# Scores of two attention heads as two 64-row tiles, spread over three steps

## Chip, cores and metric

The kernel runs on one core of one Trainium2 chip. The metric is the device time of one execution in microseconds; lower is better.

## What is computed

One inference step of a two-layer decoder trunk with 512 new prompt tokens and 8 samples that continue a cache of 2048 tokens each. Layer 1 is a gated linear attention (GLA), layer 2 a stick-breaking attention over shared keys and values. The change touches only the stick-breaking attention of the prompt tokens (16 heads of 64 features), which is, for each head:

```python
z = einsum('bqhd,bkhd->bhqk', q, k) * 64**-0.5 + bias_h
mask = k_pos[None, :] < pos[:, None]
log_keep = where(mask, log_sigmoid(-z), 0.0)
later = cumsum(log_keep, reverse=True) - log_keep
a = where(mask, exp(log_sigmoid(z) + later), 0.0)
o = einsum('bhqk,bkhd->bqhd', a, v)          # then o * silu(gate), and @ w_out
```

In the kernel `a` is the product of sigmoid(z) with a running product, taken from the right, of sigmoid(-z).

## The kernel before

Every engine has one program, written out by hand, and semaphores order them. The stages follow one another: projections and GLA, output and embedding layers, then the query, gate, K and V projections of layer 2 (`g1`, `K`, `V`), the attention of the prompt, the output product `wo1` and the last gate `ple1`. From the K stage on, TensorE also multiplies the cached value pages of the samples: `value_quad` takes four pages (512 KB each) from a ring of eight slots that SP refills; four 32-column tiles run side by side. There are 32 such groups of four; the last 16 stand in the attention stage, two per pair of heads. `sample_features` turns the result of two samples into features and stands three times in the stage or at its edge.

The attention stage works by heads. The 512 queries are four blocks of 128, and block q sees (q+1)*128 keys, so a head has 128+256+384+512 = 1280 score columns. For each head:

- **scores** (TensorE, L1954): the query block, padded with zeros over the 64 rows of the other head of its pair (`qz`, copied by ScalarE in `pair_queries`, zeroed by GpSimd), times the keys `K1T`, into banks 1 (block 1), 0 (blocks 0 and 2) and 2 (block 3). A bf16 mask matmul (L1950) goes first in each block.
- **head_sigmoids** (ScalarE, L960 and L963): sigmoid(-z) into `pcum` and sigmoid(z) into `psig`, bank by bank.
- **head_scans** and **head_products** (VectorE, L1450 and L1459): the reversed running product in `pcum`, then `psig` times `pcum`.
- **weights_back** (TensorE, L1968): ten 128x128 blocks of `psig` are turned into banks 3, 4 and the upper half of bank 1.
- **head_weights** (ScalarE, L1010 to L1012): these are copied to `pat`.
- **values** (TensorE, L1981), once per pair: `V1` times `pat` as two 64-column tiles into bank 5.
- **gate_pair** (VectorE, L1464): bank 5 times the gate `g1T`.

The order on TensorE is, for head h: scores(h+1), weights_back(h), four pages, and after an odd head values of the pair. At the end come `sample_features(3)`, the turned embedding rows of layer 2 (L1863) after the gate of the last pair, and `wo1` (L1585), whose input `g1T` is split in a high part (ScalarE, `x_hi`) and a low part (VectorE, `x_lo`).

Of the kernel before, what the change touches and what calls it, by code (L numbers as in the profile page):

```python
# [12 lines left out]
P = 128  # L13
# [39 lines left out]
X_SETS = ("A", "B", "A", "B", "B", "B", "A")  # L53
# [54 lines left out]
ZBANKS = ((1, 256, (1,)), (0, 512, (0, 2)), (2, 512, (3,)))  # L108
ZB = {0: (0, 0), 2: (0, P), 1: (1, 0), 3: (2, 0)}
# [5 lines left out]
PAIR_AT = {0: 2, 1: 3, 2: 4, 4: 5, 6: 6, 8: 7}  # L115
AB = {0: (3, 0), 1: (4, 0), 3: (4, 384), 2: (1, 256)}
AO = {0: 0, 1: 512, 3: 896, 2: 1024}
# [98 lines left out]
def build(nc, x_prompt, x_sample, state_gla, cache_k, cache_v, page_table, p_prompt, p_sample,  # L216
# [3 lines left out]
    with ExitStack() as ctx:  # L220
# [22 lines left out]
        w_hi = [new(f"w_hi{i}", [P, 1024], F32R) for i in range(2)]  # L243
        w_lo = [new(f"w_lo{i}", [P, 1024], F32R) for i in range(2)]
# [100 lines left out]
        pin1 = at("pin1", [P, TB, PLE], F32, offA)  # L345
        ps1 = at("ps1", [NS, PLE], F32, offA + size([P, TB, PLE]))
        ystage = at("ystage", [P, TB, D], F32, offB)
        ysrow = at("ysrow", [NS, D], F32, offB + size([P, TB, D]))
# [6 lines left out]
        psig = [at(f"psig{i}", [P, NZ], F32, offB + i * pz) for i in range(2)]  # L355
# [4 lines left out]
        qz = [at(f"qz{i}", [P, 2, NP_TOK], F32, off_split + (0, 2, 1, 3)[i] * 4096) for i in range(4)]  # L360
# [94 lines left out]
        def _(sp):  # L455
# [79 lines left out]
            sp.wait_ge(S("z_p"), len(ZBANKS) * SH)  # L535
# [18 lines left out]
        def _(pool):  # L554
# [66 lines left out]
            for i in range(4):  # L621
                pool.wait_ge(S("mm"), last_tile("V") - (1 if i < 2 else 0))
                nc.gpsimd.memset(qz[i][HD:P, 0, :], 0.0)
                nc.gpsimd.memset(qz[i][0:HD, 1, :], 0.0).then_inc(S("qz_zero"), 1)
# [5 lines left out]
        def _(act):  # L630
# [322 lines left out]
            def head_sigmoids(h):  # L953
                if h >= 2:
                    act.wait_ge(S("at_t"), h - 1)
                for e, (bk, cols, blocks) in enumerate(ZBANKS):
                    act.wait_ge(S("z_p"), h * len(ZBANKS) + e + 1)
                    for q in blocks:
                        c0, n = ZB[q][1], (q + 1) * P
                        nc.scalar.activation(pcum[h % 2][:, SEG[q]:SEG[q] + n], bank[bk][:, c0:c0 + n], ACT.Sigmoid,  # L960
                                             bias=nbiasbc[:, h:h + 1], scale=-HD ** -0.5)
                    p0 = PSEG[blocks[0]]
                    nc.scalar.activation(psig[h % 2][:, p0:p0 + cols], bank[bk][:, 0:cols], ACT.Sigmoid,  # L963
                                         bias=biasbc[:, h:h + 1], scale=HD ** -0.5).then_inc(S("sig_p"), 1)

            def pair_queries(i):

                if i < 4:
                    act.wait_ge(S("mm"), last_tile("V") - (1 if i < 2 else 0))
                else:  # L970
                    act.wait_ge(S("z_p"), len(ZBANKS) * 2 * (i - 3))
                nc.scalar.copy(qz[i % 4][0:HD, 0, :], q1T[0:HD, i, :])
                nc.scalar.copy(qz[i % 4][HD:P, 1, :], q1T[HD:P, i, :]).then_inc(S("qz"), 1)

            for i in range(24):
# [21 lines left out]
                if i == 23:  # L997
                    pair_queries(0)
                    head_sigmoids(0)
# [4 lines left out]
            pair_queries(1)  # L1004

            def head_weights(h):
                act.wait_ge(S("at_t"), h + 1)
                if h >= 2:
                    act.wait_ge(S("o_p"), h // 2)
                nc.scalar.copy(pat[h % 2][:, 1024:1280], bank[1][:, 256:512])  # L1010
                nc.scalar.copy(pat[h % 2][:, 512:1024], bank[4])
                nc.scalar.copy(pat[h % 2][:, 0:512], bank[3]).then_inc(S("at_act"), 1)  # L1012

            for h in range(SH):
                if h + 1 < SH:
                    head_sigmoids(h + 1)
                head_weights(h)
                if h in PAIR_AT:
                    pair_queries(PAIR_AT[h])
                if h == 12:  # L1020
                    act.wait_ge(S("z_p"), len(ZBANKS) * 12)
                    split_hi(PHASES["wo1"][0])

            act.wait_ge(S("o_p"), SH // 2)
            act.wait_ge(S("v_st"), 16)
            act.dma_start(w_up1[:, :, :], w_ple_up[1].rearrange("(k p) n -> p k n", p=P)).then_inc(S("up_in"), 16)
            act.wait_ge(S("so1_used"), NS // 2)
            act.wait_ge(S("u1_out"), KT)
            for i in range(KT):
                x_hi(5 * KT + i, g1T[:, i, :])  # L1030
# [41 lines left out]
        def _(dve):  # L1072
# [370 lines left out]
            def head_scans(h):  # L1443
                C = pcum[h % 2]
                for e, (_, _, blocks) in enumerate(ZBANKS):
                    dve.wait_ge(S("sig_p"), h * len(ZBANKS) + e + 1)
                    for q in blocks:
                        n, s = (q + 1) * P, SEG[q]
                        rev = C[:, s + n - 1:s - 1:-1] if s else C[:, n - 1::-1]
                        own.did(nc.vector.tensor_tensor_scan(rev, rev, ones[:, 0:1].to_broadcast([P, n]), 1.0,  # L1450
                                                             ALU.mult, ALU.mult))

            def head_products(h):
                A, C = psig[h % 2], pcum[h % 2]
                own.wait()
                for q in range(TB):
# [3 lines left out]
                last.then_inc(S("a_p"), 1)  # L1460
# [6 lines left out]
            head_scans(0)  # L1467
            sample_gate(1)
            head_products(0)
            for h in range(SH):  # L1470
                if h == 8:
                    sample_rows(2)
                if h % 2 == 0 and h:
                    gate_pair(h // 2 - 1)
                if h + 1 < SH:
                    head_scans(h + 1)
                    if h == 8:
                        sample_gate(2)
                    head_products(h + 1)
                if h == 12:  # L1480
# [4 lines left out]
            for i in range(KT):  # L1485
# [31 lines left out]
        def _(pe):  # L1517
# [418 lines left out]
            def scores(h):  # L1936

                i = h // 2
                if h == 0:
                    pe.wait_ge(S("evac"), last_tile("V"))  # L1940
                pe.wait_ge(S("qz"), i + 1)
                pe.wait_ge(S("qz_zero"), min(i + 1, 4))
                if h >= 2:
                    pe.wait_ge(S("at_act"), h - 1)
                for e, (bk, _, blocks) in enumerate(ZBANKS):
                    if h:
                        pe.wait_ge(S("sig_p"), (h - 1) * len(ZBANKS) + e + 1)
                    for q in blocks:
                        c0, n = ZB[q][1], (q + 1) * P
                        nc.tensor.matmul(bank[bk][:, c0 + n - P:c0 + n], identb[:], maskneg[:],  # L1950
                                         start=(q != 2), stop=False, skip_group_check=True)
                    for q in blocks:
                        c0, n = ZB[q][1], (q + 1) * P
                        last = nc.tensor.matmul(bank[bk][:, c0:c0 + n], qz[i % 4][:, h % 2, q * P:(q + 1) * P],  # L1954
                                                K1T[:, i, 0:n], start=False, stop=True, skip_group_check=True)
                    last.then_inc(S("z_p"), 1)

            def weights_back(h):

                pe.wait_ge(S("a_p"), h + 1)  # L1960
                if h:
                    pe.wait_ge(S("at_act"), h)
                for kb in (0, 1, 3, 2):
                    bk, c0 = AB[kb]
                    if bk == ZBANKS[0][0] and h + 1 < SH:
                        pe.wait_ge(S("sig_p"), (h + 1) * len(ZBANKS) + 1)
                    for q in range(kb, TB):
                        last = nc.tensor.transpose(bank[bk][:, c0 + (q - kb) * P:c0 + (q - kb + 1) * P],  # L1968
                                                   psig[h % 2][:, PSEG[q] + kb * P:PSEG[q] + (kb + 1) * P], ident[:])
                last.then_inc(S("at_t"), 1)  # L1970

            def values(i):

                pe.wait_ge(S("at_act"), 2 * i + 2)
                if i:
                    pe.wait_ge(S("u1_out"), i)
# [36 lines left out]
            for i in range(24):  # L2013
# [14 lines left out]
                if i == 23:  # L2028
                    scores(0)
# [6 lines left out]
            for h in range(SH):  # L2036
                if h + 1 < SH:
                    scores(h + 1)
                if h == 0:
                    pe.wait_ge(S("kv_out"), 16)  # L2040
                if h == 8:
                    sample_features(2)
                weights_back(h)
                value_quad(QUAD * (16 + h))
                if h % 2:
                    values(h // 2)
            sample_features(3)
# [52 lines left out]
```

## Time and profile before

| | |
|---|---|
| median of 3 runs | 896.98 us (896.32 to 899.54) |
| the profiled execution | 896.06 us, of which the span of the records is 894.3 us |
| TensorE busy | 855.4 us, 96% of the span |
| VectorE busy | 544.3 us, 61% |
| ScalarE busy | 449.9 us, 50% |
| GpSimd busy | 282.0 us, 32% |
| share of TensorE in the chain that ended last | 80% |
| memory traffic | 232.5 MB, mean 260 GB/s |

Busy time counts an engine's own instructions and not its waits. The chain is followed back from the last instruction, at each step to what released it. A matmul of 4-byte data leaves two records on TensorE, and records of a pipelined engine overlap, so the distance from start to start tells the cost and not the length of one record. A window's row gives the stretch, its length, the busy us (and instructions) of TensorE, its weight loads, VectorE, ScalarE and GpSimd, and then TensorE's granted clock as a share of full speed, the mean busy share of the DMA engines and GB/s.

### The profile page before, as it was taken

To read this page: it belongs to the slowest core of one execution; us is meant where nothing else is said; L and a number is where in the kernel's file an instruction comes from. 1 tells how busy PE (TensorE), PEld (TensorE's weight loads), DVE (VectorE), ACT (ScalarE), POOL (GpSimd) and SP (SyncE) were. 2 spreads that over 40 slices of the span, in tenths; PEclk is the share of its full clock that TensorE was granted. 3 is DMA by queue.
4 is the path that set the end of the run, shared out by engine and by line. 5 is a ranking of instruction groups with operands and counts; after the bars stand their busy time and mean duration, and the time that the engine had idled before them with its cause. 6 is when DMAs were issued, how large, how long until landed. Compare 5 with 4: busy or idle time off the path is not lost.

```text
span 894.3 us, 14799 instructions
## 1 busy us (share of the span) xinstructions
PE 855.4 (96%) x5069; PEld 596.0 (67%) x5069; DVE 544.3 (61%) x672; ACT 449.9 (50%) x1498; POOL 282.0 (32%) x150
## 2 busy tenths in 40 slices
PE   5999999999899999999999999999989999999995
PEld 3556667877654444454488877877744554899994
DVE  4455385788866879979992722312367777653643
ACT  5501382245567687758863411221387766434433
POOL 3000000957786999995830000000100000020110
PEclk9999999999999999999999999999999999999997
DMA  9898978665589998988992089988798788221202
GB/s 334 281 376 283 396 242 282 217 221 207 171 297 380 383 362 315 336 316 311 348 383 88 1 292 354 355 295 312 284 339 306 269 309 327 95 95 48 95 1 95
DMA packets 109306, 232.48 MB, mean 260 GB/s; under 512 B 7409, under 2 KB 66424, under 8 KB 109232
## 3 DMA queue, kind: packets, MB, share of 16 engines
q1 hardware_dynamic: 50736, 171.64, 52.8%
q10 hardware_dynamic: 58496, 59.90, 20.0%
q8 instruction: 40, 0.66, 0.3%
q14 instruction: 34, 0.28, 0.1%
HBM read 220.38 MB, written 11.14 MB: 259 GB/s over the span
## 4 chain that ended last, share of the span: by engine, by line
PE 80%; DMA 7%; DVE 6%; ACT 4%; issue 1%; SPq 1%; POOL 0%; ACTq 0%; DVEq 0%; POOLq 0%
PE pp L1572 18%; PE pp L1585 18%; PE pp L1588 12%; PE pp L1997 6%; PE pp L1569 4%; PE pp L1954 4%; DMA s<-in_state_gla_dram 3%; DMA slot<-in_cache_v_dram 2%; PE pp L1981 2%; PE pp L1549 2%; PE pp L1968 2%; PE pp L1600 2%; PE pp L1665 1%; PE pp L1612 1%; DMA slot<-in_w_ple_gate_dram 1%
## 5 line engine op out<-in xcount | busy, mean ns | idle before, releaser
L611 POOL TENSOR_TENSOR slot<-slot,qb 128x1024 f32<-128x1024 f32 x96 | 251.0, 2645 | 89.1 <-DMA slot<-in_cache_k_dram 53.8
L1258 DVE TENSOR_REDUCE zall<-slot 128x16 f32<-128x1024 f32 x100 | 120.1, 1214 | 23.9 <-POOL slot L611 22.8
L1081 DVE TENSOR_TENSOR w_lo<-w_raw,w_hi 128x1024 fp32r<-128x1024 f32 x57 | 79.4, 1394 | 71.5 <-ACT w_hi L661 71.3
L803 ACT ACTIVATE slot<-slot 128x64 f32<-128x64 f32 x448 | 107.1, 241 | 23.4 <-POOL slot L611 23.4
L661 ACT CAST w_hi<-w_raw 128x1024 fp32r<-128x1024 f32 x58 | 60.5, 1045 | 60.1 <-PE pp L1588 26.4
L1588 PE MATMUL pp<-xa_hi,w_hi 128*128 128x512 f32 x200 | 82.1, 411 | 4.6 <-DVE w_lo L1081 4.6
L1572 PE MATMUL pp<-xn,w_raw 128*128 128x512 f32 x192 | 84.3, 593 | 0.5 <-ACT xn L672 0.5
L803 ACT ACTIVATION_READ_ACCUMULATOR slot<-slot 128x1 f32 x448 | 84.1, 188 | 0.0
L1572 PE MATMUL pp<-xn,w_unsplit 128*128 128x512 f32 x192 | 83.9, 592 | 0.0
L1588 PE MATMUL pp<-xa_hi,w_lo 128*128 128x512 f32 x200 | 79.3, 396 | 0.0
L1588 PE MATMUL pp<-xa_lo,w_hi 128*128 128x512 f32 x200 | 79.2, 396 | 0.0
L1585 PE MATMUL pp<-xb_hi,w_hi 128*128 128x260 f32 x384 | 78.8, 286 | 0.2 <-DVE w_lo_k L1081 0.2
L1585 PE MATMUL pp<-xb_lo,w_hi 128*128 128x260 f32 x384 | 77.2, 283 | 0.0
L1585 PE MATMUL pp<-xb_hi,w_lo 128*128 128x260 f32 x368 | 74.3, 283 | 0.0
L1257 DVE TENSOR_TENSOR slot<-slot,qb 128x1024 f32<-128x1024 f32 x32 | 66.5, 2080 | 0.0
L1572 PEld LDWEIGHTS pp<-xn,w_unsplit 128*128 128x128 f32 x192 | 36.5, 190 | 44.2 <-issue 44.0
L1572 PEld LDWEIGHTS pp<-xn,w_raw 128*128 128x128 f32 x192 | 36.1, 190 | 44.4 <-issue 43.5
L1450 DVE TENSOR_TENSOR_SCAN pcum<-pcum,ones 128x256 f32<-128x256 f32 (+1 forms) x64 | 49.3, 812 | 24.8 <-ACT psig L963 24.8
L1997 PE MATMUL pp<-slot,zs 128*32 128x512 f32 x480 | 61.5, 598 | 1.6 <-DMA slot<-in_cache_v_dram 0.9
L1585 PEld LDWEIGHTS pp<-xb_hi,w_hi 128*128 128x128 f32 x384 | 59.0, 189 | 1.8 <-issue 0.8
L1585 PEld LDWEIGHTS pp<-xb_lo,w_hi 128*128 128x128 f32 x384 | 59.1, 188 | 0.0
L1585 PEld LDWEIGHTS pp<-xb_hi,w_lo 128*128 128x128 f32 x368 | 56.7, 188 | 0.0
(304 smaller groups left out, 1438.2 us busy)
## 6 DMA issues: line engine op xcount, KB each, us to landing
slot<-in_cache_k_dram SPq DMA_DIRECT2D x128, 512.0 KB, 5.9
slot<-in_cache_v_dram SPq DMA_DIRECT2D x120, 512.0 KB, 5.7
w_raw<-in_gla_w_in_dram ACTq DMA_DIRECT2D x12, 1024.0 KB, 7.1
slot<-in_gla_w_in_dram SPq DMA_DIRECT2D x24, 512.0 KB, 11.0
w_raw<-in_w_kv_dram ACTq DMA_DIRECT2D x8, 1024.0 KB, 10.4
w_raw<-in_w_ple_gate_dram ACTq DMA_DIRECT2D x6, 1024.0 KB, 5.7
s<-in_state_gla_dram SPq DMA_DIRECT2D x1, 4096.0 KB, 27.5
out_dram<-s ACTq DMA_DIRECT2D x4, 1024.0 KB, 8.4
```

What stands on the lines that cost most here:

```text
L611: nc.gpsimd.tensor_tensor(slot[s][:], slot[s][:], qb[:, (n // NPG) % 2, :], ALU.mult).then_inc(S("k_mul_pool"), 1)
L661: nc.scalar.copy(hi, raw).then_inc(S("w_hi"), 1)
L803: ins = nc.scalar.activation(part, part, ACT.Copy, accum_out=zall[:, n % NPG, b * SH + h:b * SH + h + 1])
L1081: nc.vector.tensor_tensor(lo, raw, hi.bitcast(F32), ALU.subtract).then_inc(S("w_split"), 1)
L1257: own.then(nc.vector.tensor_tensor(at, at, qb[:, b % 2, :], ALU.mult))
L1258: nc.vector.tensor_reduce(zall[:, n % NPG, b * SH:(b + 1) * SH], at.rearrange("p (h d) -> p h d", d=HD), AX.X, ALU.add).then_inc(S("k_used ...
L1450: own.did(nc.vector.tensor_tensor_scan(rev, rev, ones[:, 0:1].to_broadcast([P, n]), 1.0, ALU.mult, ALU.mult))
L1569: last = nc.tensor.matmul(pp[m % 2][:, t, 0:H2], w[:, k, :], x[:, t * H2:(t + 1) * H2], start=(k == 0), stop=(k == KT - 1))
L1572: last = nc.tensor.matmul(bank[banks_of(j)[0]], w[:, k, :], x[:, 0:NP_TOK], start=(k == 0), stop=(k == KT - 1))
L1585: last = nc.tensor.matmul(pp[m % 2][:, t, 0:H2], w[:, k, :], x[:, t * H2:(t + 1) * H2], start=(k == 0 and first), stop=(k == KT - 1 and w ...
L1588: last = nc.tensor.matmul(bank[banks_of(j)[0]], w[:, k, :], x[:, 0:NP_TOK], start=(k == 0 and first), stop=(k == KT - 1 and w is wl))
L1997: last = nc.tensor.matmul(pp[3][32 * g:32 * g + 32, t, :], zs[:, c:c + 32], slot[SLOT_OF[e0 + g]][:, t * 512:(t + 1) * 512], start=(j0 == ...
```

## The change

Scores are made for a pair of heads at once. The query is read from `q1T` directly; head 0 of the pair sits in rows 0 to 63, head 1 in rows 64 to 127, and their matmuls are 64-row tiles into different banks. A pair's scores come in three steps: block 3 into banks 0 and 2, blocks 0 and 2 into the same two, block 1 into banks 1 and 5. ScalarE and VectorE follow these steps. Four sets of `psig` are kept in place of two; the third lies over split weights (`w_hi1`, `w_lo1`), the fourth over `work` and `sqacc`, the staging row of the K and V outputs of the samples. `qz`, its copies and its memsets are gone. The order on TensorE for pair p becomes: step 0 of p, values of p-2, turned weights of head 2p-2, steps 1 and 2 of p, four pages, turned weights of head 2p-1, four pages. Turned weights of the last head go to banks 0, 2 and 1. `wo1` reads its input from the set A region and `ple1` from B (before: B and A), and the high and low parts of the first seven tiles of `wo1`'s input now stand ahead of the gate of the last pair on VectorE.

```diff
-X_SETS = ("A", "B", "A", "B", "B", "B", "A")
+X_SETS = ("A", "B", "A", "B", "B", "A", "B")
-ZBANKS = ((1, 256, (1,)), (0, 512, (0, 2)), (2, 512, (3,)))
+HSTEPS = (((3,), (0, 2)), ((0, 2), (0, 2)), ((1,), (1, 5)))
+ZCOL = {0: 0, 2: P, 1: 0, 3: 0}
+SIG_AT = {(0, 0): 1, (0, 1): 2, (1, 0): 3, (2, 0): 4, (1, 1): 5, (2, 1): 6}
+AB_LAST = {0: (0, 0), 1: (2, 0), 3: (2, 384), 2: (1, 0)}
...
-        psig = [at(f"psig{i}", [P, NZ], F32, offB + i * pz) for i in range(2)]
+        psig_at = (offB, offB + pz, off_split + 8192, off_work + 2 * size([P, T]))
+        psig = [at(f"psig{i}", [P, NZ], F32, o) for i, o in enumerate(psig_at)]
...
-            sp.wait_ge(S("z_p"), len(ZBANKS) * SH)
+            sp.wait_ge(S("at_t"), SH - 2)
             sp.dma_start(pin1[:, :, :], ...)
...
+            def sigmoids(p, e, x):
+                h = 2 * p + x
+                blocks, banks = HSTEPS[e]
+                if e == 0 and x == 0:
+                    if p:
+                        act.wait_ge(S("a_first"), p)
+                    if p >= 2:
+                        act.wait_ge(S("at_t"), 2 * (p - 1))
+                if e == 1 and p:
+                    act.wait_ge(S("a_p"), h - 1)
+                act.wait_ge(S("z_p"), 6 * p + 2 * e + x + 1)
...
+            act.wait_ge(S("kv_ss"), 64)
+            for p in range(PAIRS + 1):
+                if 0 < p < PAIRS:
+                    sigmoids(p, 0, 0)
+                    sigmoids(p, 0, 1)
+                if p:
+                    head_weights(2 * p - 2)
+                if p < PAIRS:
+                    for x in range(2):
+                        sigmoids(p, 1, x)
+                        sigmoids(p, 2, x)
+                if p == PAIRS - 2:
                     split_hi(PHASES["wo1"][0])
+                if p:
+                    head_weights(2 * p - 1)
...
+            def first_blocks(p):
+                for x in range(2):
+                    dve.wait_ge(S("sig_p"), 6 * p + SIG_AT[0, x])
+                    scans(x, (3,))
+                own.wait()
+                products(p, 0, (3,))
+                products(p, 1, (3,)).then_inc(S("a_first"), 1)
+            def other_blocks(p, x):
+                dve.wait_ge(S("sig_p"), 6 * p + SIG_AT[1, x])
+                scans(x, (0, 2))
+                dve.wait_ge(S("sig_p"), 6 * p + SIG_AT[2, x])
+                scans(x, (1,))
+                own.wait()
+                products(p, x, (0, 2, 1)).then_inc(S("a_p"), 1)
...
+            for p in range(PAIRS):
+                if p == PAIRS // 2:
+                    sample_rows(2)
+                if p:
+                    first_blocks(p)
+                if p == PAIRS // 2:
+                    sample_gate(2)
+                if p >= 2:
+                    gate_pair(p - 2)
+                other_blocks(p, 0)
+                other_blocks(p, 1)
             sample_rows(3)
-            gate_pair(SH // 2 - 1)
+            gate_pair(PAIRS - 2)
             sample_gate(3)
-            for i in range(KT):
+            for i in range(KT - 1):
                 x_lo(5 * KT + i, g1T[:, i, :])
+            gate_pair(PAIRS - 1)
+            x_lo(6 * KT - 1, g1T[:, KT - 1, :])
...
+            def scores(p, e):
+                blocks, banks = HSTEPS[e]
+                if e == 0:
+                    if p:
+                        pe.wait_ge(S("sig_p"), 6 * (p - 1) + SIG_AT[1, 1])
+                    else:
+                        pe.wait_ge(S("evac"), last_tile("V"))
+                if e == 1:
+                    pe.wait_ge(S("sig_p"), 6 * p + SIG_AT[0, 1])
+                if e == 2:
+                    if p:
+                        pe.wait_ge(S("sig_p"), 6 * p)
+                        pe.wait_ge(S("at_b1"), 2 * p - 1)
+                    else:
+                        pe.wait_ge(S("kv_out"), 16)
+                    if p >= 2:
+                        pe.wait_ge(S("u1_out"), p - 1)
+                for x in range(2):
                     for q in blocks:
+                        c1 = ZCOL[q] + (q + 1) * P
+                        nc.tensor.matmul(bank[banks[x]][:, c1 - P:c1], identb[:], maskneg[:],
                                          start=(q != 2), stop=False, skip_group_check=True)
+                for q in blocks:
+                    c0, n = ZCOL[q], (q + 1) * P
+                    for x in range(2):
+                        r = x * HD
+                        ins = nc.tensor.matmul(bank[banks[x]][:, c0:c0 + n], q1T[r:r + HD, p, q * P:(q + 1) * P],
+                                               K1T[r:r + HD, p, 0:n], start=False, stop=True, skip_group_check=True)
...
+            for p in range(PAIRS):
+                if p:
+                    scores(p, 0)
+                if p >= 2:
+                    values(p - 2)
+                if p == PAIRS // 2:
                     sample_features(2)
+                if p:
+                    weights_back(2 * p - 2)
+                scores(p, 1)
+                scores(p, 2)
+                value_quad(QUAD * (16 + 2 * p))
+                if p:
+                    weights_back(2 * p - 1)
+                value_quad(QUAD * (17 + 2 * p))
+            values(PAIRS - 2)
+            weights_back(SH - 2)
             sample_features(3)
+            weights_back(SH - 1)
+            values(PAIRS - 1)
```

## Rows read from the trace of the kernel before

**Rows 1.** Windows of the attention stage: from:to, length, then each engine.
```profile
679.30:693.10 13.80, 13.62 (x95) 7.01 (x94) 10.25 (x17) 10.38 (x22) 0.00 (x0) 1.00 0.90 319
...
665.50:750.20 84.70, 83.49 (x572) 43.97 (x570) 63.59 (x105) 61.18 (x129) 0.00 (x0) 1.00 0.86 306
```

**Rows 2.** Timeline of TensorE over one head: start, us, engine, line, operation, tiles.
```profile
679.25 0.23 PE L1950 MATMUL pp<-maskneg,identb 128*128 128x128 bf16 x1
679.32 0.65 PE L1954 MATMUL pp<-K1T,qz 128*128 128x256 f32 x2
...
681.81 1.26 PE L1968 MATMUL pp<-ident,psig 128*128 128x128 f32 x10
682.99 1.92 PE L1997 MATMUL pp<-slot,zs 128*32 128x512 f32 x16
685.10 0.22 PE L1950 MATMUL pp<-maskneg,identb 128*128 128x128 bf16 x1 [0.18 <-issue]
```

**Rows 3.** The chain that ended last, from the attention stage on: start, us, what.
```profile
643.15 0.16 PE pp L1950
...
657.51 0.22 PE pp L1950
...
690.76 2.36 PE pp L1981 x16
...
764.95 0.18 DVE g1T L1394
...
766.73 46.33 PE pp L1585 x384
```

**Rows 4.** Timeline of TensorE around the 64-row state products, and four full-array blocks.
```profile
184.16 2.00 PE L1821 MATMUL pp<-vtok,kdtok 64*128 64x256 f32 x16
186.09 0.50 PE L1588 MATMUL pp<-xa_hi,w_hi 128*128 128x512 f32 x1
...
252.41 1.89 PE L1828 MATMUL pp<-vtok,attT 128*128 128x256 f32 x8
```

**Rows 5.** Timeline of ScalarE over the sigmoids and copies of one head.
```profile
680.06 0.47 ACT L960 ACTIVATE pcum<-pp,nbiasbc 128x256 f32<-128x256 f32 x1 [3.17 <-PE pp L1954]
680.44 0.47 ACT L963 ACTIVATE psig<-pp,biasbc 128x256 f32<-128x256 f32 x1
681.04 0.84 ACT L960 ACTIVATE pcum<-pp,nbiasbc 128x128 f32<-128x128 f32 x2
...
682.34 0.70 ACT L960 ACTIVATE pcum<-pp,nbiasbc 128x512 f32<-128x512 f32 x1
...
683.48 0.40 ACT L1010 COPY pat<-pp 128x256 f32<-128x256 f32 x1
...
684.68 0.64 ACT L972 COPY qz<-q1T 64x512 f32<-64x512 f32 x1
```

**Rows 6.** Groups of VectorE by form (busy us, mean ns), then its timeline over one head.
```profile
L1450 DVE TENSOR_TENSOR_SCAN pcum<-pcum,ones 128x512 f32<-128x512 f32 x16 | 19.2, 1200 | 0.0
...
L1459 DVE TENSOR_TENSOR psig<-psig,pcum 128x512 f32<-128x512 f32 x16 | 10.9, 682 | 0.0
...
679.37 0.69 DVE L1464 TENSOR_TENSOR g1T<-pp,g1T 128x512 f32<-128x512 f32 x1 [0.71 <-PE pp L1981]
...
682.49 2.39 DVE L1450 TENSOR_TENSOR_SCAN pcum<-pcum,ones 128x128 f32<-128x128 f32 x3 [0.86 <-ACT psig L963]
684.91 1.70 DVE L1459 TENSOR_TENSOR psig<-psig,pcum 128x128 f32<-128x128 f32 x4
```

**Rows 7.** Timeline of SP's page issues.
```profile
647.76 0.33 SPq L508 DMA_DIRECT2D work<-in_cache_v_dram  x1
...
685.12 8.35 SPq L508 DMA_DIRECT2D slot<-in_cache_v_dram  x7
```

**Rows 8.** DMA issues, 643.3 to 648 and 742 to 752: KB, median landing.
```profile
work<-in_cache_v_dram SPq DMA_DIRECT2D x1, 512.0 KB, 6.0
...
slot<-in_cache_v_dram SPq DMA_DIRECT2D x7, 512.0 KB, 6.5
```

More of the change, by code:

```diff
@@ L242, in build @@
         off_split = top[0]
-        w_hi = [new(f"w_hi{i}", [P, 1024], F32R) for i in range(2)]
-        w_lo = [new(f"w_lo{i}", [P, 1024], F32R) for i in range(2)]
+        w_hi, w_lo = zip(*[(new(f"w_hi{i}", [P, 1024], F32R), new(f"w_lo{i}", [P, 1024], F32R)) for i in range(2)])
         off_work = top[0]
@@ L966, in pair_queries @@
[L966 to L973, printed above, removed]
+            def sigmoids(p, e, x):
[9 more added lines that the diff above has]
+                act.wait_ge(S("z_p"), 6 * p + 2 * e + x + 1)
+                z, A, C = bank[banks[x]], psig[2 * (p % 2) + x], pcum[x]
+                for q in blocks:
+                    c0, n = ZCOL[q], (q + 1) * P
+                    nc.scalar.activation(C[:, SEG[q]:SEG[q] + n], z[:, c0:c0 + n], ACT.Sigmoid,
+                                         bias=nbiasbc[:, h:h + 1], scale=-HD ** -0.5)
+                p0, cols = PSEG[blocks[0]], sum((q + 1) * P for q in blocks)
+                nc.scalar.activation(A[:, p0:p0 + cols], z[:, 0:cols], ACT.Sigmoid, bias=biasbc[:, h:h + 1],
+                                     scale=HD ** -0.5).then_inc(S("sig_p"), 1)
@@ L997, in _ @@
                 if i == 23:
-                    pair_queries(0)
-                    head_sigmoids(0)
+                    sigmoids(0, 0, 0)
+                    sigmoids(0, 0, 1)
                 if i >= KV_LAG + 8:
@@ L1003, in _ @@
                 kv_tile(t)
-            pair_queries(1)
             def head_weights(h):
@@ L1441, in _, with scans, products @@
                     own.did(nc.vector.memset(pcum[i][:, c:c + 1], 1.0))
[L1443 to L1456, printed above, removed]
+            def scans(x, blocks):
+                C = pcum[x]
+                for q in blocks:
+                    n, s = (q + 1) * P, SEG[q]
+                    rev = C[:, s + n - 1:s - 1:-1] if s else C[:, n - 1::-1]
+                    own.did(nc.vector.tensor_tensor_scan(rev, rev, ones[:, 0:1].to_broadcast([P, n]), 1.0,
+                                                         ALU.mult, ALU.mult))
+            def products(p, x, blocks):
+                A, C = psig[2 * (p % 2) + x], pcum[x]
+                for q in blocks:
                     n, s = (q + 1) * P, SEG[q]
@@ L1956, in scores @@
-                    last.then_inc(S("z_p"), 1)
+                for q in blocks:
+                    c0, n = ZCOL[q], (q + 1) * P
+                    for x in range(2):
+                        r = x * HD
+                        ins = nc.tensor.matmul(bank[banks[x]][:, c0:c0 + n], q1T[r:r + HD, p, q * P:(q + 1) * P],
+                                               K1T[r:r + HD, p, 0:n], start=False, stop=True, skip_group_check=True)
+                        if q == blocks[-1]:
+                            ins.then_inc(S("z_p"), 1)
@@ L1958, in weights_back @@
             def weights_back(h):
+                p, x = h // 2, h % 2
+                at = AB_LAST if h == SH - 1 else AB
                 pe.wait_ge(S("a_p"), h + 1)
[L1961 removed]
+                if h and h < SH - 1:
                     pe.wait_ge(S("at_act"), h)
                 for kb in (0, 1, 3, 2):
[L1964 to L1966 removed]
+                    bk, c0 = at[kb]
+                    if kb == 2 and x:
+                        if p + 1 < PAIRS:
+                            pe.wait_ge(S("sig_p"), 6 * (p + 1) + SIG_AT[2, 0])
+                        pe.wait_ge(S("at_b1"), h)
@@ L2028, in _ @@
                 if i == 23:
-                    scores(0)
+                    scores(0, 0)
                     sample_features(1)
```

104 lines of the change are left out of this document (25 added, 79 removed).

## Prediction

> **What bounds the kernel now.** I read four views. The windows over the attention stage come first: from 665.5 to 750.2 us TensorE is busy 83.5 of 84.7 us at full granted clock, and inside one pair of heads (679.3 to 693.1) it is busy 13.6 of 13.8 us, against VectorE 10.3, ScalarE 10.4 and the DMA engines 0.90 of their time [rows 1]. So TensorE sets the pace, but nothing else is idle by much. The timeline of TensorE gives the price of each block [rows 2]: scores with masks of one head 681.81 - 679.25 = 2.56 us, ten turned blocks 1.18, four value pages 2.11 (1.9 where nothing is waited for). The chain gives the values of a pair, 2.36, the ends of the stage (first mask 643.15, last product 766.73), and the place where the first pairs are slow (657.51) [rows 3]. The pair is then 2 x 2.56 + 2 x 1.18 + 2.1 + 1.9 + 2.36 = 13.8 us, which is the window. I expect the stages before 643 and after 766.7 unchanged: their instructions, buffers and waits stay, only two buffer regions trade names. The whole question is therefore how much earlier than 766.73 the product of the output weights starts.
>
> **TensorE's work.** Removed are 64 full-array score blocks on a query half filled with zeros; added are 64 blocks of half the rows, two of which may run side by side. The state products of the first layer have exactly this form [rows 4]: 16 records of 64 rows x 256 columns take 1.93 us from start to next start, where 8 full-array records of 256 columns take 1.89. So two 64-row tiles do overlap: one after the other, 16 records would take twice that. What remains is the price of changing the form, and it depends on what a column costs. At most it costs 1.81 ns (2.56 less four masks of 0.06, over 1280 columns); then the group's 1024 columns are 1.85 and, with 0.1 that I add for entering, 0.18 is overhead. Four passes at 2.4 GHz, the level that a granted clock of 1.00 is, would be 1.67 ns; then the columns are 1.71 and the overhead 0.33 per step. I take the second split, the dearer one. A pair has 1280 columns once, 2.13 us, eight masks at 0.06 (679.32 - 679.25), 0.45, and three steps at 0.33, 1.0: together 3.6 us instead of 5.12 (3.3 by the first split). I take steps 0, 1 and 2 as 1.3, 1.4 and 0.9. The floor for a step's overhead is nothing (saves 1.0 more a pair), the ceiling twice 0.33 (costs 1.0 more).
> The Trainium skill, "TensorEngine Tiling (Array Packing)", section Tiling Modes, says that changing the tiling mode drains the engine; it gives no price. By that rule the change pays at three places more in a pair, and the sum is the 3.6 us above; without a drain it would be 3.2. The rows of the 64-row group leave room for it and don't settle it.
> TensorE's own work per pair falls from 13.8 to 13.8 - 1.5 = 12.3 us. If that were the pace, the six steady pairs would save 9 us.
>
> **Why the pace is not 12.3.** The second half of step 2 writes bank 5, so it waits until the gate of the pair two back has been multiplied out of bank 5. VectorE does that gate behind the last score blocks (512 columns) of this pair, and those wait for ScalarE. From the start of step 0 to step 2: step 0's matmuls 1.2 and 0.27 until ScalarE reads them (a block whose columns are through at 679.80 is read at 680.06 [rows 2, 5]); four 512-column sigmoids at 0.57 (two take 683.48 - 682.34 = 1.14) and 0.15 to the end of the last (a record of 0.70 against a pace of 0.57), 2.43 [rows 5]; the second 512-column scan 1.24; two 512-column products 1.3; the gate 0.69 and 0.06 [rows 6]. Sum 7.2 us. TensorE has between those points step 0 1.3, values 2.3, ten turned blocks 1.1, step 1 1.4, that is 6.1. It stands 1.1 us in front of step 2. Then come step 2 0.9, pages 2.0, turned 1.15, pages 1.9: 5.95. The pair is 7.2 + 5.95 = 13.15 us. Before, the gate was in time.
> VectorE's other blocks (1.2 + 0.7 + 1.1 per head, 6.0 a pair) and ScalarE's rest (1.30, 0.74 and copies 1.20 per head) [rows 5, 6] are finished about 2 us before the next step 0 needs them; VectorE sums to 10.2 a pair, ScalarE to 8.8 since the query copies (1.25 a pair) are gone. They are not the bound. ScalarE's loss of the copies and GpSimd's of its memsets cost and give nothing in the steady part.
>
> **Pages.** The two page groups of a pair now stand 3.1 us apart and then 10 us apart. SP issues a page every 1.09 us (8.35 us for seven) [rows 7], so the eighth is issued 7.8 us after the first group ends; it is wanted at 13.15 + 1.2 = 14.3 us. It has 6.5 us to land. The medians are 6.0 for the last of five and 6.5 where eight pages and weights came together [rows 8]. So this is just hidden; each us beyond 6.5 adds 1 us to a pair.
>
> **The start.** 643.1 step 0 of pair 0; its four sigmoids end at 647.0. The last two K/V copies then run to 649.6. A new wait stands here: the fourth set of weights lies on the staging row of the sample outputs, so ScalarE waits for that store to land, about 3 us (estimate, between 2 and 5; pages of 512 KB take 5 to 6), until 652.6. Its four remaining sets, 4.1 us, end at 656.1, and step 0 of pair 1 waits for the third. The cover is page group 17, whose last page is issued at 647.76 and lands 6.0 later, 653.8 [rows 7, 8], and ends at 655.7; the wait alone thus costs about 0.4. Step 1 of pair 1 then waits 1.5 us for its own sigmoids, since no values stand before it: 660.0. Then step 2, pages 18, turned, pages 19 (a wait of about 1 for the last page): pair 2 begins at 668.4. The old kernel's first pairs are slow too (scores of head 2 only at 657.51 [rows 3]), so no more than 1 us is won or lost up to here.
>
> **The end.** Six pairs at 13.15 and the sample features of the middle (1.8 us, of which 1.1 fills the stall) give 668.4 + 78.9 + 0.7 = 748.0. Values of pair 6 2.3, turned 1.15, sample features 1.75, turned 1.15 bring 754.4. The turned head is copied, 1.2 plus 0.4 of handover: values of pair 7 start at 756.0 and end at 758.35. Now the gate of pair 7 is queued on VectorE behind seven low parts of the output's input, and these follow seven high parts on ScalarE which start after the last copy: 755.9 + 7 x 0.54 = 759.7, the last low part at 760.9 and the gate at 761.6. The embedding's turned rows (1.5 us, from 764.95 + 0.2 to 766.73 [rows 3]) end at 763.1. TensorE idles 3.2 us there. I take 762.8 +- 0.6 for the product's start.
>
> **Sum.** 766.73 - 762.8 = 3.9 us. The profiled execution before took 896.06 us (span 894.3), 0.9 below the median of the runs, 896.98. I forecast 893.0 for the median. No change from measurement noise is told apart within 0.5%, 4.5 us: this forecast lies just inside it.
>
> **Rivals.** (1) The stall in front of step 2 doesn't occur, because the chain of 7.2 is shorter by the 1.1: pace 12.1 to 12.3, six pairs save 5 to 6 more, and 887.5 comes out. For it: ScalarE's and VectorE's rows are from overlapped runs, and 0.27 and 0.15 are my handovers. Against: scans and products are sums of rows. 0.12. (2) Slower side: pages. Eight now come in 7.6 us in place of 9.1, while the DMA engines are at 0.90. If the last lands after 7.2 us instead of 6, a pair is 13.8 and nothing is won (897); at 8 us it is 14.5 and the stage ends 2.5 us later, 899. Against: the mean load only rises to 319 GB/s x 13.8 / 13.15 = 335. Chance 0.18. (3) The change doesn't do what it says: the two tiles run one after the other. Then a pair gets 2.1 us longer, 15.2, and the kernel takes about 904. The 64-row group speaks against it [rows 4]. 0.04. (4) The clock falls in the idle of 3 us at the end; the clock is 1.00 in all windows shown [rows 1], and the 46 us product would show it: 0.02.
> My forecast's own mechanism has 0.64, with its own range 890.0 to 895.5 (step overhead 0.1 lower or higher moves six pairs by 1.8, the store's wait up to 1.3, the handovers about 1).
>
> **Numbers.** Faster by over 0.5% (below 892.5): all of rival 1 and under half of the forecast's 0.64: 0.41. Slower by over 0.5% (above 901.5): rival 3, the tail of rival 2, some of 4: 0.08. Within: 0.51. The range 887.5 to 899.0 takes in rival 1's value and rival 2's up to a landing of 8 us.
>
> **What would show it.** Score blocks as 64x128 records, 128 of them, half of them starting within some ns of the other half, steps of 1.3, 1.4 and 0.9; a pair period of 13.1 to 13.3; a wait of about 1 us of step 2's masks on VectorE's gate; VectorE idle 2 us before the first scan; page groups without a wait on a DMA from pair 2 on; TensorE idle 1.6 before the last values and 3 before the embedding, on the gate. Wrong would be: page waits in the steady pairs, a period below 12.6 or above 13.8, or a time outside of the stage that moves.

## The result, and the profile after

The changed kernel takes 901.12 us in the median of 20 runs against 896.98 for the kernel before: ratio 1.0042, 95% interval 1.0028 to 1.0055. One execution of the twenty stood far off at 2184 us and is left out of the ratio; without it the median is 900.6. The forecast was 893.0 with a range up to 899.0, so the time lies outside the range. The change is 0.4% slower where 0.4% faster was forecast.

The profiled execution took 896.67 us (span 894.9), the fastest of the twenty, about 4 us below their median; it is read for where time goes, not for the total. TensorE's timeline over one steady pair (start, us, engine, line, operation, tiles; in brackets the idle time before and what ended it):

```profile
670.79 0.29 PE L1980 MATMUL pp<-maskneg,identb 128*128 128x128 bf16 x2
671.01 1.13 PE L1986 MATMUL pp<-K1T,q1T 64*128 64x512 f32 x4
672.07 2.38 PE L2020 MATMUL pp<-pat,V 128*64 128x512 f32 x16
674.37 1.31 PE L2005 MATMUL pp<-ident,psig 128*128 128x128 f32 x10
675.52 0.39 PE L1980 MATMUL pp<-maskneg,identb 128*128 128x128 bf16 x4
675.84 1.14 PE L1986 MATMUL pp<-K1T,q1T 64*128 64x128 f32 x8
678.01 0.27 PE L1980 MATMUL pp<-maskneg,identb 128*128 128x128 bf16 x2 [1.03 <-DVE g1T L1485]
678.21 0.70 PE L1986 MATMUL pp<-K1T,q1T 64*128 64x256 f32 x4
678.84 1.92 PE L2036 MATMUL pp<-slot,zs 128*32 128x512 f32 x16
680.70 1.31 PE L2005 MATMUL pp<-ident,psig 128*128 128x128 f32 x10
...
683.80 0.28 PE L1980 MATMUL pp<-maskneg,identb 128*128 128x128 bf16 x2
```

This is the pair as it was forecast. The scores are 64*128 records: block 3 of both heads, 512 columns each, takes 1.13 us. In the kernel before, the same block of one head alone took 1.08:

```profile
680.89 1.08 PE L1954 MATMUL pp<-K1T,qz 128*128 128x512 f32 x2
```

The steps are 1.28 (670.79 to 672.07), 1.46 (675.52 to 676.98, where the wait of 1.03 begins) and 0.83 (678.01 to 678.84) against my 1.3, 1.4 and 0.9. Step 2 stands 1.03 us on the gate against my 1.1. The pair is 683.80 - 670.79 = 13.01 us against 13.15.

What is not as forecast shows in what TensorE waited for from the first mask to the product of the output weights. Each row has the group that waited, what ended the wait, the us in total, how often, and the longest:

```profile
PE pp L1980 <- DVE g1T L1485: 5.2, 5, 1.0
PE pp L2036 <- DMA work<-in_cache_v_dram: 4.9, 4, 1.9
PE pp L1886 <- DVE g1T L1485: 3.2, 1, 3.2
PE pp L1980 <- ACT psig L969: 2.7, 2, 1.4
PE pp L2036 <- DMA slot<-in_cache_v_dram: 1.5, 1, 1.5
PE pp L2020 <- ACT pat L1009: 1.4, 1, 1.4
```

Rows 1, 3, 4 and 6 were in the forecast. Rows 2 and 5 are 6.4 us of waits for value pages, for which I had allowed 1. The chain that ended last runs through three of these landings (start, us, what); the one in the middle of the stage, at 715.76, is read further below, and these are the others:

```profile
661.85 6.95 DMA work<-in_cache_v_dram
...
743.57 6.30 DMA work<-in_cache_v_dram
```

And the windows, first over a stretch of the start, then over the first 8 us of the product of the output weights (engines as in [rows 1], then granted clock, DMA share, GB/s):

```profile
649.00:661.00 12.00, 8.41 (x68) 3.57 (x66) 6.89 (x14) 7.65 (x17) 0.00 (x0) 1.00 1.02 408
```
```profile
766.90:775.00 8.10, 8.10 (x55) 8.10 (x56) 1.76 (x2) 0.00 (x0) 0.00 (x0) 0.79 0.01 2
```

In the first the DMA engines are full, with a share of 1.02 and 408 GB/s. In the second the clock is 0.79, a mean of full speed and of half speed (1.2 GHz) for 3.4 us; the product takes 47.86 us from 766.88 by the chain, where it took 46.33 [rows 3]. The low clock begins behind the last and longest idle place of the stage, 3.24 us.

The stage from its first mask to the first matmul of the product is what compares executions, since what lies ahead of it differs from profile to profile: the first mask stands between 642.3 and 649.0 us in the profiles of this study. It took 766.66 - 643.09 = 123.6 us before and 766.81 - 642.25 = 124.6 after (125.1 and 125.8 in two more profiles, below).

### The profile page after: what moved, and what is told of

The parts are those of the page before. It is cut to its first block, busy times and chain, and to the rows that moved or that the text cites. A ratio compares the mean times of both kernels' runs of the same rounds, so it can differ in the third digit from the quotient of the medians.

```text
span 894.9 us, 14766 instructions
## 1 busy us (share of the span) xinstructions
PE 845.6 (94%) x5069; PEld 587.8 (66%) x5069; DVE 545.5 (61%) x672; ACT 441.2 (49%) x1482; POOL 278.1 (31%) x142
## 4 chain that ended last, share of the span: by engine, by line
PE 74%; DVE 9%; DMA 8%; ACT 4%; SPq 3%; issue 2%; POOL 1%; ACTq 0%; DVEq 0%; POOLq 0%
PE pp L1608 20%; PE pp L1595 18%; PE pp L1611 11%; PE pp L2036 5%; PE pp L1592 4%; DMA s<-in_state_gla_dram 3%; DMA work<-in_cache_v_dram 2%; PE pp L1572 2%; PE pp L1623 2%; PE pp L1688 1%; SPq L503 1%; DMA slot<-in_cache_k_dram 1%; PE pp L1635 1%; DVE w_lo L1089 1%; PE pp L1986 1%
## 5 line engine op out<-in xcount | busy, mean ns | idle before, releaser
L1456 DVE TENSOR_TENSOR_SCAN pcum<-pcum,ones 128x512 f32<-128x512 f32 (+3 forms) x64 | 49.2, 812 | 25.4 <-ACT psig L969 25.3
```

## Experiments

Every kernel was timed in five rounds against the kernel before on the same chip. All but the control start from the changed kernel.

**The changed kernel again**, twice, as the base for the others. No edit.

> The changed kernel once more, as the base of this call. Theory A (the page ring cannot follow two page groups in a burst, and TensorE's clock is halved for some us after the idle places): 898 to 903, product of the output weights starting at 766 or later, waits on pages of 5 to 10 us in total, and a spell of half clock near the start of that product. Theory B (the pair loop itself is slower than I summed): pairs without a page wait of 13.5 or more. The first profile shows 13.0 to 13.1 for such pairs, so B would need this run to differ.

> The changed kernel as the base of this call: 900 to 902, as in its earlier runs (901.1 and 900.5).

Measured: 900.45 (ratio 1.0038, 1.0022 to 1.0054) and 901.84 (1.0052, 1.0034 to 1.0069). The result repeats. The stages are 125.1 and 125.8 us, with page waits of 6.6 and 6.5 us in five places each. In the first the clock stays full at the product:

```profile
771.80:780.00 8.20, 8.20 (x69) 8.20 (x69) 1.92 (x2) 1.44 (x5) 0.00 (x0) 1.00 0.05 9
```

So the half clock there is not in each execution. In the second it is there again, for 6.8 us.

**Half of each page** of the attention stage.

```diff
-                sp.dma_start(slot[s][:], src[...])
+                w = D // 2 if n >= NPAGES + 4 * 16 else D
+                sp.dma_start(slot[s][:, 0:w], src[...][:, 0:w])
...
-                    slot[SLOT_OF[e0 + g]][:, t * 512:(t + 1) * 512],
+                    slot[SLOT_OF[e0 + g]][:, (0 if m0 >= 64 else t * 512):(512 if m0 >= 64 else (t + 1) * 512)],
```

> Left out: of the value pages loaded in the attention stage only the first half of the columns is loaded, and TensorE multiplies that half twice; its instructions are the same. Theory A: no waits on pages in the stage, pairs of 13.0 to 13.2 throughout, pair 2 at 668.4 and the product of the output weights at about 763, which is 4 us less than the changed kernel's fastest profile and more against its median; 892 to 895, and less scatter. Theory B or a cause outside of the pages: unchanged, 899 to 902. If only the clock after the 3 us idle at the end matters, the time is 896 to 899 with the half clock spell still there.

Measured: 894.10 (890.31 to 899.31), ratio 0.9960 (0.9942 to 0.9978). The stage is 118.3 us. TensorE's page waits:

```profile
PE pp L2037 <- DMA work<-in_cache_v_dram: 1.1, 1, 1.1
...
PE pp L2037 <- DMA slot<-in_cache_v_dram: 0.7, 1, 0.7
```

The stall on the gate (5.1 us in five) and the idle before the embedding (3.2) are as they were. With most of the page waits out of the way (1.8 us are left) the kernel is 3.8 us faster than the kernel before, close to the 4.0 of the forecast. The full pages cost 6.4 us of the median. Not all of this is in waits named for pages: against the first base these shrink by 4.8 us, and TensorE's waits for ScalarE in the start by 1.5, since ScalarE waits 1.6 us for the store of the staging row here and 3.8 in the changed kernel.

**The same cut in the kernel before**, the control.

> The kernel before, with the cached value pages of the attention stage cut to their first 512 columns (the other half is not loaded, TensorE multiplies the loaded half twice). It leaves out half of the value pages' data for the last samples. Theory 1 (the new order is what waits for pages: the kernel before had them hidden): its own page waits are short, so the median falls by at most 1.5 us, ratio 0.998 to 1.000, against the 6.4 us that the same cut gave the changed kernel. Theory 2 (both kernels wait for pages alike, and the change only lost its gain elsewhere): the cut gives this one about as much, 4 us or more, ratio below 0.996.

Measured: 897.05 against 897.07, ratio 1.0000 (0.9986 to 1.0015); the stage is 123.5 us (765.81 - 642.27) against 123.6. Theory 1 holds: the old order had every page hidden, and the new order made the wait. In neither of the two profiles of the old order does TensorE wait for a page in the stage, so the cut gives nothing.

**A smaller store in the start.**

```diff
-  act.dma_start(v_prompt[0].rearrange("(b p) h d -> p b (h d)", p=P), V1[:, :, :])
+  act.dma_start(v_prompt[0].rearrange("(b p) h d -> p b (h d)", p=P)[:, 0:1, :], V1[:, 0:1, :])
```

> The changed kernel, with only the first quarter of the new V rows of the prompt stored (0.5 MB of 2 MB; the other three quarters of that output are left out). Theory 1 (the page waits of the first two pairs, 0.9 to 1.9 us each, come from the 2 MB that are stored in the same 10 us as the pages land): these waits shrink to under half, pair 2 begins 1.5 to 2.5 us earlier, ratio to the kernel before about 1.002. Theory 2 (pages alone, issued in bursts of eight, are late whatever else moves): the waits stay within 0.5 us each, and the median stays within 1.5 us of the changed kernel's, ratio 1.004.

Measured: 898.08, ratio 1.0014 (1.0001 to 1.0028), about 2.5 us less than the base by the ratios (2.2 to 3.4; the base was not timed again beside it). Pair 2 begins 26.6 us behind the first mask (671.24 - 644.65) instead of 28.5 (670.79 - 642.25). The two page waits before pair 2 are 1.08 and 1.06 us where three of 4.3 together stood, and all page waits of the stage fall from 6.4 to 3.6 us:

```profile
PE pp L2036 <- DMA work<-in_cache_v_dram: 3.6, 4, 1.1
```

```profile
650.00:662.00 12.00, 8.83 (x69) 3.68 (x67) 6.18 (x14) 6.49 (x15) 0.00 (x0) 1.00 0.88 316
```

The DMA engines now have room in the start. So of the page cost of 6.4 us some 2.5 come from the store that lands beside the pages. This is nearer to theory 1: pair 2 is 1.9 us earlier, and the ratio of 1.002 is inside the interval. But the waits before pair 2 shrink to half in sum, and of the three one is gone, one is nearly halved and one is 0.2 us longer. The rest of the cost stays with the pages alone. The kernel before has the same store in its start, and waits for no page there.

**The store later.** Its four blocks are issued one by one in pairs 1 to 4.

```diff
-                if t == 15:
-                    act.dma_start(v_prompt[0]..., V1[:, :, :]).then_inc(S("v_st"), 16)
...
+                if 0 < p < 5:
+                    b = p - 1
+                    act.dma_start(v_prompt[0]...[:, b:b + 1, :], V1[:, b:b + 1, :]).then_inc(S("v_st"), 16)
```

> One edit: the 2 MB store of V, issued at 649 in the changed kernel, is cut in four and issued after pairs 1 to 4. Theory A: the pages of groups 18 and 19 land 2 to 3 us earlier and pair 2 begins at 668 instead of 670.9, but each of the next pairs has 0.5 MB more in the burst, so pairs 2 to 5 may wait on pages; 0 to 2 us less in all. If the first pairs are late because of the store of the sample rows (ScalarE's wait of 3.8 us) and not the pages, that wait shrinks as well since it then lands alone, and pair 1 begins 1 us earlier.

Measured: 903.22, ratio 1.0065 (1.0039 to 1.0091), 2.8 us worse than the base. The start does get shorter (pair 2 begins 669.91 - 643.70 = 26.2 us behind the first mask, 2.3 earlier), but the pairs behind it lose it again: the waits for `work` pages are six, 6.8 us together, of which 4.4 stand behind the start of pair 2, where the changed kernel has 2.1. The stage is as long as in the bases, 125.6 us. The store found no free place in pairs 1 to 4, and moving it only moved the wait. The profile also has a half clock of 6.8 us at the product; what else makes the median 2.8 us worse is not shown.

**The gate of the last pair first.**

```diff
-            for i in range(KT - 1):
-                x_lo(5 * KT + i, g1T[:, i, :])
             gate_pair(PAIRS - 1)
-            x_lo(6 * KT - 1, g1T[:, KT - 1, :])
+            for i in range(KT):
+                x_lo(5 * KT + i, g1T[:, i, :])
```

> One edit: on VectorE the gate of the last pair stands ahead of the low parts of the output weights' input, as it did before the change. Theory A with the idle before the embedding as its own term: this idle shrinks from 3.2 to about 0.9 us (2.3 us), and if the half clock spell comes from it, 1.7 us more are won: 897 to 898 in the median against 901 for the changed kernel. If the low parts, now later, feed the product too slowly, the product gets longer than 46.3 us by over 1 us and nothing is won.

Measured: 896.97, ratio 0.9987 (0.9968 to 1.0006), 3.5 us less than the base. The last values and the embedding's turned rows, in the changed kernel and then in this one:

```profile
759.74 2.37 PE L2020 MATMUL pp<-pat,V 128*64 128x512 f32 x16 [1.44 <-ACT pat L1009]
765.36 0.63 PE L1886 MATMUL pp<-ident,pin 128*128 128x128 f32 x4 [3.24 <-DVE g1T L1485]
```
```profile
767.08 2.37 PE L2019 MATMUL pp<-pat,V 128*64 128x512 f32 x16 [1.44 <-ACT pat L1009]
770.34 0.63 PE L1885 MATMUL pp<-ident,pin 128*128 128x128 f32 x4 [0.89 <-DVE g1T L1485]
```

The idle falls by 2.35 us. The other 1.1 us fit the clock, though no run separates them. Over all profiles of this study, the half clock stood at or just ahead of the product in five of the seven with the 3.2 us of idle, and in none of the four with 0.9.

**The page groups apart.** The second group of a pair goes behind step 0 of the next one, except from pairs 3 and 7.

```diff
             for p in range(PAIRS):
                 if p:
                     scores(p, 0)
+                if p not in (0, PAIRS // 2):
+                    value_quad(QUAD * (15 + 2 * p))
                 if p >= 2:
                     values(p - 2)
...
                     weights_back(2 * p - 1)
-                value_quad(QUAD * (17 + 2 * p))
+                if p in (PAIRS // 2 - 1, PAIRS - 1):
+                    value_quad(QUAD * (17 + 2 * p))
```

> One edit in TensorE's order: the second page group of a pair is moved behind step 0 of the next pair (except around the middle sample features and at the end), so the two groups start some 5 and 7 us apart instead of 3 and 10, and one of them fills the place where step 2 waited for the gate. The bytes and the number of page issues are the same. Theory A (the burst is what the ring can't follow, not the bytes): waits on pages from pair 2 on fall to under 1 us in total except for the two places where the groups stay together, the stall of 1.03 us before step 2 is gone, pairs of 12.1 to 12.5, 894 to 897. Rival (the bytes per pair are the limit: at 12.2 us a pair needs 344 GB/s): page waits come back as the pairs get shorter, pairs stay at 13.0 or above, 899 to 901.

Measured: 898.91, ratio 1.0016 (1.0004 to 1.0029), 2.9 us less than its base. The waits:

```profile
PE pp L2036 <- DMA work<-in_cache_v_dram: 4.2, 4, 1.6
PE pp L1980 <- ACT psig L969: 3.9, 1, 3.9
...
PE pp L1980 <- DVE g1T L1485: 1.1, 1, 1.1
```

The stall on the gate is gone in four of five places, because the page group stands before it, and a steady pair takes 12.6 us, with a page wait of 0.7 in it, in place of 13.0. The page waits are 5.6 us in all (these and 1.4 for pages in `slot`), and a hole of 3.9 us opens in the start, where the group of pair 0 had been the cover for ScalarE's wait; the clock halved at its end, for 3.4 us:

```profile
654.00:663.00 9.00, 5.09 (x31) 1.15 (x24) 6.61 (x13) 6.30 (x14) 0.00 (x0) 0.81 1.02 392
```

Neither theory came out as written. The pairs got shorter, against the rival, but from the start of pair 2 on 2.5 us of page waits are left at other places than the two where the groups stay together, against under 1. So spacing the groups does not take the waits away, and the median of 898.9 lies between the two.

**Apart and gate first**, both edits.

> Both the spaced page groups and the last gate ahead of the low parts. If the two are separate terms they add: 3.5 us (as gate_first won against its base) below apart, 891 to 894, and faster than the kernel before the change by 0.5 to 0.7%. If they share a cause (idle TensorE, half clock), less than 2 us below apart.

Measured: 895.68, ratio 0.9977 (0.9957 to 0.9998), 3.2 us less than the groups apart alone, where gate first gave 3.5 by itself. The terms add.

**Half pages and gate first**, both edits.

> Left out: half of the bytes of the stage's value pages, as in half_pages; and the last gate ahead of the low parts. It is the changed kernel without page waits and without the idle place at the end. Separate terms: half_pages was 6.35 below its base and gate_first 3.5 below it, so 9 to 10 us below the base, 891. If both had won by the same half clock spell: 893 or more.

Measured: 890.78 (889.22 to 891.73), ratio 0.9921 (0.9905 to 0.9936); the stage is 115.9 us (762.84 - 646.98). It is 11.1 us below its base, where the two edits alone gave 6.4 and 3.5. The whole change in order and form is thus worth 7 us against the kernel before when next to nothing is late beside the gate's stall (1.7 us of page waits are left).

**Apart, except the group of pair 0; gate first.**

```diff
-                if p not in (0, PAIRS // 2):
+                if p not in (0, 1, PAIRS // 2):
...
-                if p in (PAIRS // 2 - 1, PAIRS - 1):
+                if p in (0, PAIRS // 2 - 1, PAIRS - 1):
```

> The changed kernel with the second page group of a pair moved behind step 0 of the next pair, except in pairs 0, 3 and 7, and with the gate of the last pair ahead of the low parts. Against the version that also moved the group of pair 0 (895.7 us, with 4.8 us of idle TensorE near 655 and half clock for 3.4 us behind it), theory 1 (that idle is a hole that the group of pair 0 fills): the idle falls to about 3 us in two parts, the clock stays, and the median is 893.5 to 895, ratio 0.995 to 0.997. Theory 2 (the pages of the next groups are then late by as much as the hole was long): 895 to 897, ratio 0.997 to 0.999.

Measured: 893.35 (888.84 to 895.94), ratio 0.9952 (0.9933 to 0.9972). It is the best version that leaves nothing out, 3.7 us below the kernel before and some 7 to 8 below the changed one. The stage is 119.8 us (767.64 - 647.82). What is left in it is pages:

```profile
PE pp L2035 <- DMA work<-in_cache_v_dram: 5.5, 6, 1.9
PE pp L2035 <- DMA slot<-in_cache_v_dram: 3.6, 3, 1.7
PE pp L1979 <- ACT psig L969: 2.1, 2, 1.3
```

Theory 1 holds in the main: the idle in the start is 1.1 us on a page and 2.1 us on ScalarE, and the clock stays full there. Nine waits for pages take 9.1 us: with the stall gone TensorE asks for them earlier. The profiled execution took 895.89 us, 2.5 above the median, so this may be more than most have. The page landings look like the next bound; no run with half pages was made of this version.

## Why the prediction was wrong

- **TensorE's work**: right. The two tiles overlap, and the steps measure 1.28, 1.46 and 0.83 us, 3.57 together against 3.6. Rival 3 is out. A pair's work without the stall is 13.01 - 1.03 = 12.0 us; the 12.3 that I wrote does not fit my own blocks either, which add up to 6.1 + 5.95 = 12.05. Nor does the 3.2 for steps without a drain: columns and masks alone are 2.13 + 0.45 = 2.6.
- **The stall before step 2 and the pair of 13.15**: right, 1.03 us in five pairs and 13.0 to 13.1 us. Rival 1 is out.
- **Pages**: this step failed, "It has 6.5 us to land" and "So this is just hidden". From the issue of the last of eight pages to the moment TensorE wanted it there were 6.0 to 6.2 us in pairs 3, 5 and 7, and in these pages took 6.1, 7.65 and 6.3. In pairs 2, 4 and 6, each behind a late page or the sample features, there were 7.2 to 7.6 us, and they took 5.8 to 6.9. I took medians of the kernel before (6.0 and 6.5) as if a landing did not scatter, in an order that leaves no margin. In the kernel before, the last of four pages was issued 8.4 us ahead of its use (start, us, engine, line, operation, tiles) and took 6.1:

```profile
680.43 0.33 SPq L508 DMA_DIRECT2D work<-in_cache_v_dram  x1
...
688.85 0.62 PE L1997 MATMUL pp<-work,zs 128*32 128x512 f32 x1
```

  In pair 3 of the changed kernel the last of eight pages took 6.1 us as well, but it was issued 6.2 us ahead of its use, and was only just in time:

```profile
688.82 0.33 SPq L510 DMA_DIRECT2D work<-in_cache_v_dram  x1
...
695.07 0.62 PE L2036 MATMUL pp<-work,zs 128*32 128x512 f32 x1
```

  Two pairs later it was not. SP's issues of that burst:

```profile
708.10 6.90 SPq L510 DMA_DIRECT2D slot<-in_cache_v_dram  x7
715.76 0.33 SPq L510 DMA_DIRECT2D work<-in_cache_v_dram  x1
```

  The eighth page is issued 7.66 us behind the first. The chain has the same page:

```profile
715.76 7.65 DMA work<-in_cache_v_dram
723.54 1.92 PE pp L2036 x16
```

  It was wanted 6.1 us behind its issue and landed after 7.65, and TensorE stood 1.71 us. The landing times of the eight pages are 3.5, 4.6, 5.5, 6.9, 7.1, 7.3, 7.5 and 7.65 us. The last five land every 1.27 us while the issues come every 1.09 (512 KB in 1.27 us are 413 GB/s, and the windows' busiest row shows 408), so there a page takes 0.18 us longer than the one before. But that is 0.7 us of the growth of 4.2. The other 3.5 come in the first four pages, which land 2.0 to 2.5 us apart while the DMA engines are not full (share 0.80, 268 GB/s):

```profile
708.10:715.80 7.70, 7.70 (x61) 3.87 (x61) 6.81 (x13) 5.26 (x12) 0.00 (x0) 1.00 0.80 268
```

  Why they land so far apart, and why the burst of one pair ends after 5.8 us and that of another after 7.65, stays open. In the four pairs from pair 2 on without a page wait the last page was there 0.1 to 1.9 us before its use. The 1.09 us of an issue was right, though 8.35 us for seven is not its source: that row has a pause of 1.5 us in it. The kernel before takes four pages in turn 5.8 and 8.0 us after the last four. TensorE waited for none of them in the stage.
  The Trainium skill, "DMA: Bandwidth & Descriptors", section "Where 436 GB/s comes from", puts the ceiling of the ports at 435 GB/s and says that for traffic from memory some 358 GB/s bind. The trace shows 408 over 12 us, above the second figure and under the first. By the first, an estimate, a burst would land a page every 1.21 us; the last pages of this one land every 1.27.
- **The start**: "pair 2 begins at 668.4" was 25.3 us behind the first mask; it was 28.5. With half pages it is 24.7 (668.55 - 643.87). The waits for the staging row's store (3.8 us on ScalarE against my 3) and for pair 1's sigmoids were priced well enough. The 3.2 us are page waits of 0.85, 1.52 and 1.92, 4.3 where I had allowed 1, in a stretch where the 2 MB store lands too. I had listed neither that store nor its 2 MB among what the pages compete with.
- **The end**: right. Idle of 1.44 and 3.24 us against 1.6 and 3.2; 14.9 us (751.93 to 766.81) from the values of pair 6 to the product against about 15. My own sum gave 763.1 and I wrote 762.8, without a reason. Of the 3.2 us of idle the gate's place in VectorE's queue makes 2.35, and the run with the gate first won 3.5 us in the median.
- **The clock**: rival 4, given 0.02, happened in the profiled execution, at a price of 1.5 us (47.86 - 46.33), and in four more profiles. The windows shown of the kernel before had 1.00, and its longest idle place in the stage was 1.75 us. The rows for a longer one were missing, and 0.02 was too little for a gap that I had myself forecast at 3.2 us.
- **Rival 2** named the mechanism at 899 for 8 us of landing. It came out otherwise than written there, since the waits stand in the start and in two later pairs and not in each pair. Its chance of 0.18 was too low, and its top was summed wrongly: a pair of 14.5 is 0.7 us over the 13.8 that gave 897, six pairs are 4.2 us, so the top of the range should have been 901 and not 899. That the measured 901.1 is near this is chance: the waits that make it are others, and a part of the time is the clock.

The account against the forecast, in ratios: 1.0042 measured, 893.0 / 896.98 = 0.9956 forecast. Of these 0.86% the full pages are 1.0038 - 0.9960 = 0.78%, by the half pages and their base.

About 1 us stays open, and it seems to lie ahead of the stage. In the half pages with the gate first the stage is 7.7 us shorter than before and what follows it 0.6 us shorter (127.1 against 127.7), but the median only 7.1. In the best version it is 3.7 and 1.2 (126.5), and the median 3.7. The first mask stands at 645.8 us in the mean of the eleven profiles with the new order, and at 643.1 and 642.3 in the two with the old. So the stages before 643, which I expected unchanged, may have lost a us or more. But single profiles spread from 642.3 to 649.0 there, and no run tells a cause. On one chip the mean granted clock is 0.987 over 12 executions of the changed kernel and 0.989 over 31 of the kernel before.

## What to carry to other kernels

When TensorE gets faster or its order changes, ask of each transfer that was hidden whether it still is. For the last page of each burst, take the time from its issue to its use in both orders (here 8.4 and 6.2 us), and hold it against the longest landing of the trace and not against the median. The profile of the kernel before already had landings of 6.9 us. The full rate of the DMA engines does not tell enough: a first landing of 3.5 us and seven more pages at 1.27 would be 12.4 us, and the burst above took 15.3. Put every other transfer of that stretch, stores too, into the account. Cutting the bytes in half in both kernels tells whether the pages are the new bound. A short instruction that TensorE waits for should stand ahead of long elementwise work in its queue; and work without dependencies (here four pages) is best put exactly where the stall is, as long as its own data is there.

## What was not expected of the hardware

- In the profile of the changed kernel the last four pages of each burst of eight land 1.16 to 1.29 us apart, mostly 1.27 (413 GB/s), with issues every 1.09. The first ones land up to 3.5 us apart, and the last page of a burst took from 5.8 to 7.65 us.
- After an idle of 3.2 us TensorE ran at half clock for 3.4 to 6.8 us in five of seven profiles, and at the same place in two not; after 3.9 and 4.8 us (the groups apart, with and without the gate first) it did in both.
